# Two transformer blocks: first norm tile by tile, norms reordered, S5 taps by row halves in pairs, output slots filled later

## The reference

```python
# block 1
h = rms_norm(x, mix_norm_pre)
m = hybrid_mixer(h)       # z = h @ w_in -> q, k, v, xr, gr; dilated attention of 8 heads;
                          # conv + gated linear recurrence (LRU) * gelu(gr); concat @ w_out
x = x + rms_norm(m, mix_norm_post)
h = rms_norm(x, mlp_norm_pre)
x = x + rms_norm(relu(h @ w_ff_in) ** 2 @ w_ff_out, mlp_norm_post)
# block 2; mod = silu(c) @ ada_w + ada_b, split into sh1, sc1, g1, sh2, sc2, g2
hn = rmsnorm(x, mix_pre_g) * (1 + sc1) + sh1
proj = hn @ w_in_2        # gated linear attention (GLA), and the S5 state-space layer
h = x + g1 * rmsnorm(concat(gla, s5) @ w_out_2, mix_post_g)
hn2 = rmsnorm(h, ffn_pre_g) * (1 + sc2) + sh2
out = h + g2 * rmsnorm(moe(hn2), ffn_post_g)   # 4 of 32 experts per token
```

## Time and profile before

| | us |
|---|---|
| median of 3 runs | 2246.59 |
| lowest, highest | 2235.36, 2247.24 |
| profiled execution | 2245.24 |
| its span | 2243.5 |
| TensorE busy in the span | 2107.9 |
| VectorE busy | 1703.1 |
| ScalarE busy | 1294.0 |
| GpSimd busy | 219.3 |

### The profile page before, as it was taken

One profiled execution on the slowest core, in us unless ns is written; L12 is line 12 of the kernel. 1 busy time (PEld: TensorE's weight loads), 2 busy tenths in 40 slices (PEclk: granted clock), 3 DMA queues, 4 the chain that ended last, 5 costly groups with the idle time before them and its releaser, 6 DMA issues.

```text
span 2243.5 us, 28761 instructions
## 1 busy us (share of the span) xinstructions
PE 2107.9 (94%) x10524; PEld 1731.8 (77%) x10524; DVE 1703.1 (76%) x1459; ACT 1294.0 (58%) x1194; POOL 219.3 (10%) x188
## 2 busy tenths in 40 slices
PE   6999889999998998699999999999999999999982
PEld 6774578888887777678888888888888888888871
DVE  5944553333344755789999999999999999999995
ACT  5335352322243343367777777777777777777761
POOL 1020000000000030230101111111110111111102
PEclk9998899999998999599999999999999999999995
DMA  5479422232225332499999999999999999999965
GB/s 195 144 207 400 164 75 93 95 103 99 99 94 146 104 129 85 152 320 403 373 399 378 389 384 386 387 375 395 378 391 389 376 396 378 389 384 385 386 271 196
DMA packets 172539, 610.80 MB, mean 272 GB/s; under 512 B 18688, under 2 KB 19584, under 8 KB 168608
## 3 DMA queue, kind: packets, MB, share of 16 engines
q1 hardware_dynamic: 148576, 541.10, 64.6%
q0 software_dynamic: 13344, 44.75, 5.6%
q10 hardware_dynamic: 10560, 24.12, 3.0%
HBM read 568.87 MB, written 41.06 MB: 272 GB/s over the span
## 4 chain that ended last, share of the span: by engine, by line
PE 82%; DVE 10%; ACT 3%; DMA 2%; issue 2%; POOL 0%; DVEq 0%; ACTq 0%; POOLq 0%; SPq 0%
PE ps L1954 24%; PE ps L1956 24%; PE ps L1955 24%; PE ps L2392 1%; PE ps L2375 1%; PE ps L2384 1%; DMA plain<-in_ada_w 1%; PE ps L2127 1%; DVE scr L1907 1%; DVE scr L1535 1%; PE ps L2107 1%; DVE x_res L1539 1%; DVE scr L1198 1%; PE ps L2098 0%; DMA scr<-in_exp_w_down 0%
## 5 line engine op out<-in xcount | busy, mean ns | idle before, releaser
L1954 PE MATMUL ps<-split,spare 128*128 128x512 f32 x872 | 344.4, 395 | 6.8 <-DVE spare L1826 6.8
L1955 PE MATMUL ps<-split,spare 128*128 128x512 f32 x872 | 341.8, 392 | 0.0
L1956 PE MATMUL ps<-split,spare 128*128 128x512 f32 x872 | 341.6, 392 | 0.0
L1752 DVE TENSOR_TENSOR split<-scr,split 128x2048 fp32r<-128x2048 f32 x140 | 317.1, 2286 | 28.9 <-ACT split L1084 28.8
L1084 ACT ACTIVATE split<-scr 128x2048 fp32r<-128x2048 f32 x140 | 264.2, 1911 | 60.8 <-PE ps L1956 58.8
L1244 DVE TENSOR_TENSOR split<-ring,split 128x2048 fp32r<-128x2048 f32 x54 | 123.6, 2290 | 201.4 <-ACT split L800 201.3
L800 ACT ACTIVATE split<-ring 128x2048 fp32r<-128x2048 f32 x54 | 103.1, 1910 | 193.7 <-PE ps L1956 183.1
L1954 PE MATMUL ps<-actT,spare 128*128 128x512 f32 (+1 forms) x484 | 185.2, 383 | 18.8 <-DVE actL L1211 18.8
L1954 PEld LDWEIGHTS ps<-split,spare 128*128 128x128 f32 x872 | 165.2, 189 | 41.8 <-issue 6.2
L1956 PEld LDWEIGHTS ps<-split,spare 128*128 128x128 f32 x872 | 164.8, 189 | 34.7
L1955 PEld LDWEIGHTS ps<-split,spare 128*128 128x128 f32 x872 | 165.0, 189 | 34.1
(11 more groups left out here) (460 smaller groups left out, 4226.2 us busy)
## 6 DMA issues: line engine op xcount, KB each, us to landing
scr<-in_exp_w_gu SPq DMA_DIRECT2D x208, 1024.0 KB, 8.5
ring<-in_exp_w_gu SPq DMA_DIRECT2D x72, 1024.0 KB, 6.5
scr<-in_exp_w_down SPq DMA_DIRECT2D x72, 1024.0 KB, 10.5
ring<-in_exp_w_down SPq DMA_DIRECT2D x68, 1024.0 KB, 9.8
plain<-in_ada_w SPq DMA_DIRECT2D x24, 1024.0 KB, 8.4
ring<-in_w_in SPq DMA_DIRECT2D x18, 1024.0 KB, 6.0
y_slots<-scr ACTq DMA_DIRECT2D x35, 512.0 KB, 8.5
ring<-in_w_ff_in SPq DMA_DIRECT2D x16, 1024.0 KB, 5.2
```

The costliest lines, as they stand in the source:

```text
L1752: tt(r32(low), raw(o % RAW), high, ALU.subtract).then_inc(S("low"), 1)
L1954: mm(o, stat[0], mov[0], start=start, stop=False)
L1955: mm(o, stat[0], mov[1], start=False, stop=False)
L1956: return mm(o, stat[1], mov[0], start=False, stop=stop)
```

## The change

1. Norm 1: SyncE asks for two token tiles, the small vectors (`cols`), weight piece 0, the other two tiles and piece 1, in this order. GpSimd writes `eps` first, and ScalarE no longer waits for all constants but for `eps` alone; it takes a root of `eps` (`sqrt_next`) before the first tile. Each tile is squared, scaled and transposed before the next is squared; tiles 2 and 3 are transposed between the products of `first_column`. Scaled rows no longer share two buffers. GpSimd's zero fills of the S5 responses wait for piece 1.
2. The S5 table stage on VectorE: the sixteen small copies of powers move ahead of the wait for the stored turn table; `split_low(7)` moves between the two halves of the input table; `attention_bias` is cut in two, and its second half and the lambda chain come behind the copies of the taps. ScalarE does `split_high(9)` before it copies xr and the S5 transposes.
3. The S5 taps: each q4 has both row halves in turn, in two banks.
4. The fill of `y_slots` waits until the first column of the feed-forward (`f1`, 3) is done.
5. Norms 2 and 3: another `sqrt_next` ahead of norm 2; one square over both banks of a tile in `post_squares` (norm 4 too), eps as the root's bias; another order of the steps on ScalarE and VectorE; the transposes of tiles 0 and 1 one step earlier in `by_row`, those of tile 3 after k = 4, not 6; and in norm 3 the gain and shift in one instruction for each block of 128 channels.

Left out below: the views of the buffers, the removed helper `norm_out`, and blank lines.

```diff
     keys += [("s5b", n) for n in range(8)]
-    keys += [("s5k", par, q4) for par in range(2) for q4 in range(4)]
+    keys += [("s5k", par, q4) for q4 in range(4) for par in range(2)]
     keys += [("gr", m) for m in range(4)]
...
         def _(sp):
-            for i in range(NT):
+            def load_x(i):
                 sp.dma_start(x_res[:, i, :], a["x"][0, i * P:(i + 1) * P, :]).then_inc(S(f"x_or_ada_in{i}"), 16)
-            sp.dma_start(cols[:], a["cols"]).then_inc(S("cols_in"), 16)
...
+            load_x(0)
+            load_x(1)
+            sp.dma_start(cols[:], a["cols"]).then_inc(S("cols_in"), 16)
             load_piece(0)
+            load_x(2)
+            load_x(3)
+            load_piece(1)
             for dst, src in ((par, a["s5_par"]), (b_r, a["s5_b_re"]), (b_i, a["s5_b_im"]), (c_r, a["s5_c_re"]),
...
                 sp.dma_start(dst, src).then_inc(S("s5_small_in"), 16)
-            load_piece(1)
             small = [(s5_d[:], a["s5_d"]), (w_gate[:, 0], a["w_rgate"]),
...
             step = stepper(pool, "pool_step")
+            nc.gpsimd.memset(eps[:], EPS).then_inc(S("eps_ready"), 1)
             step(nc.gpsimd.memset(ident[:], 0.0))
...
             pool.wait_ge(S("constants"), 1)
+            pool.wait_ge(S("piece_in1"), 16)
             for q8 in range(2):
...
+            full(pool, ("f1", 3))
             pool.dma_start(y_slots[NE * P:, :].rearrange("(s b) (h d) -> s (b h) d", s=P, h=4),
...
-            act.wait_ge(S("constants"), 1)
+            act.wait_ge(S("eps_ready"), 1)
+            def sqrt_next():
+                step(af(st[:, ST_N - 1:ST_N], eps[:, 0:1], ACT.Sqrt))
+            sqrt_next()
             first_squares = lambda i: squares(1, i, junk, S(f"x_or_ada_in{i}"), 16)
             first_squares(0)
+            norm_rows(1, 0)
             first_squares(1)
-            norm_rows(1, 0)
-            first_squares(2)
             norm_rows(1, 1)
             norm_high(1, 0)
+            split_high(0)
+            norm_high(1, 1)
+            first_squares(2)
+            norm_rows(1, 2)
             first_squares(3)
-            norm_rows(1, 2)
-            norm_high(1, 1)
-            split_high(0)
+            split_high(1)
             norm_rows(1, 3)
-            split_high(1)
             norm_high(1, 2)
...
             split_high(8)
+            split_high(9)
             act.wait_ge(S("bx_ready"), 1)
...
             af(att_bias, cnt_t, ACT.Ln).then_inc(S("att_log"), 1)
-            split_high(9)
             act.wait_ge(S("lam_ready"), 1)
...
             split_high(early[0])
+            sqrt_next()
...
-                c = [st[:, ST_PS + 2 * i + n:ST_PS + 2 * i + n + 1] for n in range(2)]
+                c = st[:, ST_PS + 2 * i + 1:ST_PS + 2 * i + 2]
                 for n in range(2):
-                    bank = full(act, key(i, n))
-                    step(af((junk if s == 3 else junk_2)[:, 0:HALF], bank, ACT.Square, scale=D ** -0.5, accum_out=c[n]))
-                step(af(c[0], c[0], ACT.Identity, bias=eps[:, 0:1]))
-                af(c[1], c[1], ACT.Sqrt, bias=c[0]).then_inc(S("post_root"), 1)
+                    full(act, key(i, n))
+                bank, both = plan[key(i, 0)][0], junk if s == 3 else junk_2
+                step(af(both.rearrange("p (n d) -> p n d", n=2), ps[:, bank:bank + 2, :], ACT.Square, scale=D ** -0.5,
+                        accum_out=c))
+                af(c, c, ACT.Sqrt, bias=eps[:, 0:1]).then_inc(S("post_root"), 1)
...
                 after(0)
+                norm_rows(s + 1, 0)
                 after(1)
-                norm_rows(s + 1, 0)
                 post_squares(s, 2, key)
                 norm_rows(s + 1, 1)
+                norm_high(s + 1, 0)
+                after(2)
+                norm_high(s + 1, 1)
+                norm_rows(s + 1, 2)
                 post_squares(s, 3, key)
-                norm_high(s + 1, 0)
-                norm_high(s + 1, 1)
-                after(2)
-                norm_rows(s + 1, 2)
                 split_high(n)
...
                     bank = ps[:, plan[key][0], :].rearrange("p (k n) -> p k n", n=P)
-                    out_of(key, tt(y[:, 4 * h:4 * h + 4], bank, over(gain[:, 4 * h:4 * h + 4], 2, P), ALU.mult))
+                    if shift is None:
+                        ins = tt(y[:, 4 * h:4 * h + 4], bank, over(gain[:, 4 * h:4 * h + 4], 2, P), ALU.mult)
+                    else:
+                        for k in range(4 * h, 4 * h + 4):
+                            ins = ts(y[:, k], bank[:, k % 4], gain[:, k:k + 1], shift[:, k:k + 1], ALU.mult, ALU.add)
+                    out_of(key, ins)
                 for h in range(2):
                     copied(dve, ("norm", s, i, h))
-                if shift is not None:
-                    tt(y, y, over(shift, 2, P), ALU.add).then_inc(S("norm_out"), 1)
-                else:
-                    dve.sem_inc(S("norm_out"), 1)
+                dve.sem_inc(S("norm_out"), 1)
...
             norm_inverse(1, 1)
-            norm_out(1, 0, gain)
+            norm_gain(1, 0, gain)
+            norm_low(1, 0)
+            norm_gain(1, 1, gain)
+            split_low(0)
+            norm_low(1, 1)
             norm_inverse(1, 2)
-            norm_out(1, 1, gain)
-            split_low(0)
             norm_inverse(1, 3)
-            norm_out(1, 2, gain)
             split_low(1)
-            norm_out(1, NT - 1, gain)
-            def attention_bias():
+            for i in (2, 3):
+                norm_gain(1, i, gain)
+                norm_low(1, i)
+            def attention_counts():
...
+            def attention_bias():
...
             step(tt(ca_r, c9r, a9r, ALU.mult))
+            for j in range(SL):
+                cp(pw_t[:, j, :], ar[:, SL - 1 - j, :])
+                ins = cp(pw_th[:, j, :], ai[:, SL - 1 - j, :])
+            step(ins)
             dve.wait_ge(S("turn_stored"), 16)
...
             step(tt(ca_t, c9i, a9r, ALU.mult))
-            step(stt(ca_n, ca_n, -1.0, ca_t, ALU.mult, ALU.subtract))
-            for j in range(SL):
-                cp(pw_t[:, j, :], ar[:, SL - 1 - j, :])
-                ins = cp(pw_th[:, j, :], ai[:, SL - 1 - j, :])
-            ins.then_inc(S("ca_ready"), 1)
+            stt(ca_n, ca_n, -1.0, ca_t, ALU.mult, ALU.subtract).then_inc(S("ca_ready"), 1)
             dve.wait_ge(S("ca_ready"), 1)
...
             step(tt(bx_r, bx_r, tmp8, ALU.subtract))
+            split_low(7)
             step(tt(bx_i, b8r, a8i, ALU.mult))
...
             tt(bx_i, bx_i, tmp8, ALU.add).then_inc(S("bx_ready"), 1)
-            split_low(7)
             split_low(8)
-            attention_bias()
+            attention_counts()
             split_low(9)
...
+            for q4 in range(4):
+                for par_ in range(2):
+                    key = ("s5k", par_, q4)
+                    bank = full(dve, key)[0:SC, :].rearrange("p (q n) -> p q n", q=4)
+                    out_of(key, cp(taps[0:SC, q4 // 2, par_, 4 * (q4 % 2):4 * (q4 % 2) + 4, :], bank))
+            attention_bias()
...
             dve.wait_ge(S("small_in"), 16 * N_SMALL)
-            for par_ in range(2):
-                for q4 in range(4):
-                    key = ("s5k", par_, q4)
-                    bank = full(dve, key)[0:SC, :].rearrange("p (q n) -> p q n", q=4)
-                    out_of(key, cp(taps[0:SC, q4 // 2, par_, 4 * (q4 % 2):4 * (q4 % 2) + 4, :], bank))
             for par_ in range(2):
...
-            def post(s, i, key, gain, done):
+            def post(s, i, key, gain, done, beside=None):
...
                     copied(dve, key(i, n))
+                if beside is not None:
+                    norm_inverse(s + 1, beside)
                 tt(x_res[:, i, :], x_res[:, i, :], tmp.rearrange("p n d -> p (n d)"), ALU.add).then_inc(S(done), 1)
...
-                after = lambda i: post(s, i, key, post_gain, done)
+                after = lambda i, beside=None: post(s, i, key, post_gain, done, beside)
                 after(0)
-                after(1)
-                norm_inverse(s + 1, 0)
+                after(1, 0)
                 norm_inverse(s + 1, 1)
+                norm_gain(s + 1, 0, gain, shift)
                 after(2)
-                norm_gain(s + 1, 0, gain, shift)
                 norm_gain(s + 1, 1, gain, shift)
                 norm_low(s + 1, 0)
+                norm_inverse(s + 1, 2)
                 norm_low(s + 1, 1)
-                norm_inverse(s + 1, 2)
                 after(3)
...
                             ins.then_inc(S("split_used"), 1)
-                        if not th and s > 1 and k in (1, 6):
+                        if not th and k in (1, 4):
                             transposes(s, NT - 2 if k == 1 else NT - 1)
-                        if not th and s == 1 and k == 1:
-                            transposes(s, NT - 1)
...
                         ins.then_inc(S("split_used"), 1)
+                    if s == 3 and (h, i) == (0, NT - 1) or s < 3 and (h, i) == (1, NT - 2):
```

(35 more changed lines are left out.)

8 lines of the change are left out of this document (2 added, 6 removed).

## The result

| | before | after |
|---|---|---|
| median, us | 2245.38 (4 runs) | 2209.87 (4 runs) |
| lowest, highest | 2235.36, 2247.24 | 2206.17, 2215.40 |
| profiled execution, its span | 2245.24, 2243.5 | 2209.39, 2207.7 |

A forecast was written before the change was run, and what follows sets the result against it. TensorE, busy 2107.9 of 2243.5 us, was taken as the bound, so only its waits and low clock count. 13.2 + 7.6 + 8.0 + 10.4 - 0.2 = 39.0 us saved gave a median of 2208 us, range 2197 to 2228.

The forecast's parts named there:

- A: Start to end of S5 taps: earlier first product, no piece 7 wait, paired taps; 13.2 us saved (4 to 15).
- the 4.9 us wait: TensorE's 4.86 us wait for weight piece 7 would go, and 1.7 us of low clock behind it.
- B: Attention without the zero fill: waits for modulation weights (2.6 us) and low clock (5.0 us) go; 7.6 us saved.
- The cover in the feed-forward: First feed-forward: weight loads may be some 12 us late before anybody waits, so the moved fill costs nothing there.
- Rival 3: Slower: the fill blocks a feed-forward weight load by more than 12 us, costing 48 us, 2256 us; chance 0.05.
- C: Norm 2: first wait shorter by 3.9 us, second wait and its low clock gone; 8.0 us saved (3 to 9).
- D: Norm 3: cheaper gain and shift, shorter first wait, second wait and its clock gone; 10.4 us saved (4 to 11.5).
- the rest: Behind norm 3: norm 4's joined square makes the first root at most 0.3 us late; -0.2 us.
- Rival 1: Waits shrink but the clock does not come back and VectorE gives back more: 22 us saved, 2225 us; chance 0.26.
- Rival 2: S5 taps: the row halves don't run side by side, 6.5 us less saved, 2214 us; chance 0.06.

The follow-up runs named there:

- two steps: Changed kernel with norm 3's gain and shift made as two products and then one add again: 2211.46 us.
- shared: Changed kernel with norm 3's gain and shift split, VectorE making channels 0 to 511 of each tile and ScalarE the others: 2206.94 us.
- piece 9 late: Changed kernel with ScalarE's high half of weight piece 9 behind the copies of xr and of the S5 transposes again: 2213.39 us.

## Why the prediction was right, and where it was not

**What bounds it, and A to the end of the taps.** Right in each step, none more than 0.5 us off: the first product, its lead eaten in the k and v columns (1.8 us left, 1.5 on average over ten profiles, 1.5 forecast), the 4.9 us wait and its clock gone (experiment: a wait of 3.96 us is back when one low half is put back), the taps (13.72 and 7.16 us). One reason was wrong: the high half of piece 9 ahead buys nothing; the experiment found no wait at piece 9.

**B: the fill.** Forecast 7.6, trace 9.9: TensorE is idle 1.8 us less, the rest is clock. That the low clock followed the waits for the weights was the assumption, and it does not hold: the fill put back gave nine waits and full speed, and three kernels without the fill (two steps, shared, piece 9 late) had the 10 us of half speed at about 195 us all the same. There it stands behind a wait of 2.28 us for ScalarE; of the other profiles with the late fill, which have the same wait, three had 3.4 us of half speed behind it and six had none. Over twelve profiles without the early fill the stretch from the attention to w_out's product is 85.4 us on average (83.4 to 89.0); with it, 93.3 and 93.7. So the fill costs 8 us by these profiles (9 us by the medians in the kernel before, 4 to 6 in the changed one), and the 9.9 of this pair of profiles hangs on where half speed fell. That is luck, not the mechanism that was forecast. What sets it is open.

The cover in the feed-forward held, though less easily than I had it. Transfers of the changed kernel: the fill, then the weight pieces in the stretch of the earlier trace rows.

```profile
DMA to landing us min/median/max: 33.6/33.6/33.6
```
```profile
DMA to landing us min/median/max: 5.0/5.3/14.5
```

One piece landed in 14.5 us, where the prediction wanted below 11: 9.3 us late of the 12 that the prefetch covers. TensorE waited for none. Rival 3 decides from 12 us, and was 2.7 us away.

**C.** 7.2 of 8.0 us. The experiments show the parts: the order of the steps 2.2 us of the first wait and all of the second, the root ahead 1.2 us.

**D: the step that failed.** "Eight instructions on 128 elements; sixteen such took 3.22 us, so 1.65 us a tile" was taken from rows of another form; the eight take 2.65 us. They differ in two things: the operand is in PSUM, and there are two values per partition (gain and shift) instead of one. Rows of VectorE's TENSOR_SCALAR in the changed kernel (ns min/median/max): the eight's form; the sixteen's, with one value per partition; with a constant; then 512 elements from SBUF with two values and with a constant; from PSUM with one value and with a constant.

```profile
L1215 DVE TENSOR_SCALAR scr<-ps,st,cols x32: 401/404/415, 636.9 to 662.2; 128x128 f32<-128x128 f32 x32
L1614 DVE TENSOR_SCALAR scr<-ident,st x16: 278/282/284, 664.9 to 667.9; 128x128 f32<-128x128 f32 x16
L1816 DVE TENSOR_SCALAR scr<-scr x1: 226/226/226, 896.1 to 896.1; 128x128 f32<-128x128 f32 x1
...
L1455 DVE TENSOR_SCALAR scr<-scr,cols x4: 541/542/547, 133.2 to 141.6; 128x512 f32<-128x512 f32 x4
L1283 DVE TENSOR_SCALAR post_g<-post_g x1: 427/427/427, 114.1 to 114.1; 128x512 f32<-128x512 f32 x1
...
L1656 DVE TENSOR_SCALAR scr<-ps,cols x2: 744/745/746, 728.9 to 729.5; 128x512 f32<-128x512 f32 x2
L1595 DVE TENSOR_SCALAR scr<-ps x32: 681/682/685, 318.8 to 472.9; 128x512 f32<-128x512 f32 x32
```

Each value per partition costs about 0.06 us (282 - 226; half of 542 - 427; 745 - 682). So of the 0.12 us between 404 and 282, half is the second value and about half is left for PSUM: 0.5 us a tile each, 1.0 in all. Two tiles stand ahead of the first product: 2 x 1.0 = 2.0 us, which is 4.88 - 2.8. That the wait follows these two tiles one for one is what the experiment in two steps shows (2 x 0.24 us there, 0.47 us of the wait); a tile at 1.65 us was not run. The two steps that I priced at 2.5 us a tile cost 2.54, so the fusion lost 0.24 us a tile. The Trainium skill (VectorE: DVE Perf Modes, Why PSUM operands drop a tier) says that f32 from PSUM runs at the slowest tier; I stated that D would be 1 us smaller by it and kept it out of the sum. The trace bears out its direction, and the 0.5 us a tile that I estimated from it is about the size of PSUM's half; the other half I had not seen.

Behind the first product 6.4 us were forecast and 4.0 came: of the second wait 0.90 us stays, and the clock gave 1.5 us, not 2.7, because half speed behind the longer first wait lasted 6.2 us, where the kernel before had 5.8. The other 0.4 us is not traced. D gave 6.2 us of 10.4.

**The sum.** 39.0 forecast, 35.8 in the trace; 35.5 between the medians. A's miss is +0.3, B's +2.3, C's -0.8, D's -4.2 and the rest's -0.8. In the profiles B's surplus covers half of D's miss; the medians, which do not hang on one profile, are 3.5 us short of the forecast. The rest's -0.8 is the clock: behind the 2.81 us wait in the GLA stage this profile has 6.8 us of half speed that the profile before has not, which makes that stretch 1.0 us longer (28.50 against 27.51). The median 2209.87 lies nearer to the forecast than the sum does, 2.3 us above 2207.6, only because the median before has come down from 2246.59 to 2245.38 since.

Rival 1 (the clock does not come back) was right at norm 3's first wait and in the GLA stage. One reason against it was a wrong reading: a dip does stand behind a wait under 1 us outside the attention, 751.4 to 754.8 in the kernel before, 2 us behind a wait of 0.68 us. Rival 2 fell: 13.72 against 7.16 us. Two of the prediction's sums do not come out: with A and D at their upper ends the low side of the range is about 2205, not 2197, and rival 2's 0.06 at 2214 belongs to "faster" whole, which makes it 0.92 at the least.

## What to carry to other kernels

Follow a wait by the chain of the engine that ends it; a step moved ahead is worth what the next in that chain lets through (here 1.5 to 1.8 of 5.0 us), and one left in front of it, like the reciprocal ahead of tile 1's low half, takes all of it back. Price a new instruction by a row with the same size, the same operand memory and as many values per partition: 3.22 us for sixteen from SBUF with one value each became 2.65 us for eight from PSUM with two. A background fill costs least where each transfer has slack, but measure the longest landing, not the median: 14.5 against 5.3 us. One profile does not price a change of a few us where the clock moves: the same stage took 83.4 to 89.0 us.

## What the runs showed of the hardware that was not expected

- The same wait did not always bring the same low clock. Of twelve profiles of the changed kernel and its variants, the wait of 2.81 us in the GLA stage came with half speed in six (3.4 or 6.8 us long) and without in six; where it came, the next wait fell from 3.1 to 1.2 or 1.5 us, so the stretch over both waits grew by 1.0 us at most (27.5 to 28.5). Behind the wait for piece 7 the kernel before had 3.4 us of half speed (a wait of 4.86 us), the same kernel with the late fill, which is the same program up to there, 6.8 us (4.82 us).
- The same products up to the S5 transposes, started at the same time, took up to 1.4 us more or less from profile to profile. The lasting full speed began between 22.2 and 25.3 us in these ten profiles, and the transposes came later by about half of that (113.69 us with 22.2, 115.05 with 25.3).
- A value per partition in VectorE's TENSOR_SCALAR costs about 0.06 us, at 128 elements as at 512 (226 and 282 ns; 427 and 542 ns for two).
- The fill of 8 MB took 60.6 us beside the modulation weights and 33.6 us beside the feed-forward's.
